# The opening of a two-block transformer kernel: the input in four column quarters between the halves of the first weights, those weights split by row blocks, products in another order

## What is computed

```python
h = rmsnorm(x, g_pre[i])        # x (1, 256, 1024); rmsnorm scales each row, then multiplies by the gain
proj = h @ w_in[i]              # w_in (1024, 3792)
(qa, ka, va, gate_a, qi, ki, wi, qb, kb, vb, fb, gate_b) = jnp.split(proj, offs, axis=-1)
```

## Time and profile before

| | us |
|---|---|
| median of 3 runs | 816.74 |
| lowest, highest | 814.30, 816.82 |
| the profiled execution, device time | 814.75 |
| its span | 812.9 |
| TensorE busy | 798.4 |

### The profile page before, as it was taken

How to read it: one execution, slowest core, us unless ns; L and a number is a source line. 1 busy time by engine, 2 the same in 40 slices (tenths; PEclk the granted TensorE clock), 3 DMA queues, 4 the chain that set the end, 5 groups by cost and what they waited for, 6 DMA issues and landing times.

```text
span 812.9 us, 11157 instructions
## 1 busy us (share of the span) xinstructions
PE 798.4 (98%) x4190; PEld 664.5 (82%) x4190; DVE 538.1 (66%) x728; ACT 415.6 (51%) x586; POOL 112.7 (14%) x144
## 2 busy tenths in 40 slices
PE   8999999999999999999999999999899999999998
PEld 6998987778878778888888888887567888888886
DVE  5647988767585766566656556677975766665661
ACT  5546556554655554364444444545665545444440
POOL 1600300000020510030000000079900000000000
PEclk9999999999999999999999999999999999999999
DMA  8951444346747633646655655464214466655541
GB/s 314 322 191 40 156 156 156 119 156 223 241 145 238 208 106 104 207 156 207 206 191 175 202 194 172 151 206 131 78 53 156 156 207 211 209 199 190 175 151 52
DMA packets 76503, 140.43 MB, mean 173 GB/s; under 512 B 2953, under 2 KB 22609, under 8 KB 76465
## 3 DMA queue, kind: packets, MB, share of 16 engines
q1 hardware_dynamic: 74352, 134.03, 49.8%
q0 software_dynamic: 1968, 5.82, 2.3%
q10 hardware_dynamic: 144, 0.07, 0.0%
HBM read 138.86 MB, written 1.05 MB: 172 GB/s over the span
## 4 chain that ended last, share of the span: by engine, by line
PE 90%; DVE 5%; ACT 2%; DMA 1%; issue 1%; POOL 0%; SPq 0%; ACTq 0%; DVEq 0%
PE bank L1737 56%; PE bank L2093 13%; PE bank L2095 7%; PE bank L1885 2%; PE bank L1803 2%; PE bank L2097 2%; DVE w_lo L1176 2%; PE bank L1946 2%; PE bank L1772 1%; PE bank L1855 1%; PE bank L1920 1%; DMA raw<-in_w_in 1%; DVE tok L1348 1%; PE bank L1751 1%; DMA raw<-in_w_mem_kv 1%
## 5 line engine op out<-in xcount | busy, mean ns | idle before, releaser
L1737 PE MATMUL bank<-w_hi,a_both 128*128 128x512 f32 (+2 forms) x752 | 233.6, 382 | 0.4 <-PE bank L1737 0.4
L1176 DVE TENSOR_TENSOR w_lo<-raw,w_hi 128x2048 fp32r<-128x2048 f32 (+2 forms) x65 | 146.0, 2247 | 53.8 <-ACT w_hi L725 53.3
L1615 DVE TENSOR_TENSOR w_lo<-raw,w_hi 128x2048 fp32r<-128x2048 f32 x48 | 110.0, 2292 | 91.9 <-ACT w_hi L1075 91.0
L2093 PE MATMUL bank<-a_both,w_hi 128*128 128x512 f32 x448 | 161.4, 399 | 0.0
L1737 PEld LDWEIGHTS bank<-w_hi,a_both 128*128 128x128 f32 x752 | 140.7, 188 | 22.0 <-issue 1.1
L725 ACT ACTIVATE w_hi<-raw 128x2048 fp32r<-128x2048 f32 (+2 forms) x64 | 120.7, 1888 | 59.7 <-PE bank L1737 35.6
L1075 ACT ACTIVATE w_hi<-raw 128x2048 fp32r<-128x2048 f32 x48 | 92.1, 1918 | 112.5 <-PE bank L1737 53.7
L1737 PE MATMUL bank<-w_hi,b_hi 128*128 128x512 f32 x376 | 148.7, 395 | 0.1
L1737 PE MATMUL bank<-w_hi,b_lo 128*128 128x512 f32 x376 | 146.5, 390 | 0.0
L1737 PE MATMUL bank<-w_lo,b_hi 128*128 128x512 f32 x376 | 146.5, 390 | 0.0
L1737 PE MATMUL bank<-w_lo,a_both 128*128 128x512 f32 (+2 forms) x376 | 141.7, 377 | 0.0
(11 more groups left out here) (242 smaller groups left out, 859.6 us busy)
## 6 DMA issues: line engine op xcount, KB each, us to landing
raw<-in_w_ff SPq DMA_DIRECT2D x64, 1024.0 KB, 5.1
raw<-in_w_in_moba SPq DMA_DIRECT2D x20, 512.0 KB, 4.4
raw<-in_w_merge SPq DMA_DIRECT2D x8, 1024.0 KB, 5.1
raw<-in_w_out SPq DMA_DIRECT2D x8, 1024.0 KB, 5.1
m<-in_w_in SPq DMA_DIRECT2D x6, 880.0 KB, 9.1
raw<-in_w_in SPq DMA_DIRECT2D x5, 880.0 KB, 8.5
raw<-in_w_mem_kv SPq DMA_DIRECT2D x4, 1024.0 KB, 5.2
raw<-in_w_ple_gate SPq DMA_DIRECT2D x4, 1024.0 KB, 5.0
```

The costliest lines, as they stand in the source:

```text
L1176: dve.tensor_tensor(w_lo[:, v % RING, 0:n], landing[land_slot(v)][:, 0:n], w_hi[:, v % RING, 0:n].bitcast(F32), ALU.subtract).then_inc(lo_ ...
L1615: dve.tensor_tensor(w_lo[:, (base + c) % RING, :], raw[:, (base + c) % RAW, :], w_hi[:, (base + c) % RING, :].bitcast(F32), ALU.subtract). ...
L1737: ins = pe.matmul(banks[t][:, 0:n], xa[:, kt, ts], wa[:, slot, w], start=first and k == 0 and q == 0, stop=last and k == kts - 1 and q == 2)
L2093: pe.matmul(b_hid[f][:, :].rearrange("p (q n) -> p q n", q=2), w_hi[:, slot, w], both_, start=kt == 0, stop=False)
```

## The change

- x comes in four column quarters instead of two halves by two token tiles: one transfer covers both token tiles of 256 columns, in 1 KB rows. Order on SP: quarter 0, row blocks 0 and 1 of unit 0, quarter 1 (its own semaphore `x_second_landed`), row blocks 2 and 3, quarters 2 and 3, then unit 1 as before.
- g_pre is loaded by ScalarE, behind the identity, instead of by GpSimd.
- ScalarE casts row blocks 0 and 1 of unit 0 in two instructions of 440 columns, and raises `half_ready` after each.
- TensorE transposes only group 0 ahead of the first products. Unit 0 then goes: hi products of row blocks 0 and 1; transposes of group 1; lo products of row blocks 0 and 1; hi, then lo products of row blocks 2 and 3; transposes of groups 2 and 3; w_lo products. Unit 1 keeps its order.

```diff
@@ -312,7 +312,7 @@
         memk_made, memq_made, moba_made = sem("memk_made"), sem("memq_made"), sem("moba_made")
         early_landed, half_rstd, x_half = sem("early_landed"), sem("half_rstd"), sem("x_half")
         half_landed, half_ready, pre_landed = sem("half_landed"), sem("half_ready"), sem("pre_landed")
-        x_upper_landed = sem("x_upper_landed")
+        x_upper_landed, x_second_landed = sem("x_upper_landed"), sem("x_second_landed")
         tile_done, x_tile = sem("tile_done"), sem("x_tile")
 
         merged, x_post, z_made = sem("merged"), sem("x_post"), sem("z_made")
@@ -501,21 +501,22 @@
                 for u in range(first, last):
                     load(u, land_slot(u), unit_source(u), unit_size(u))
 
-            def load_x(c):
-
-                for t in range(NT):
-                    sp.dma_start(x[:, t, c * CB:c * CB + CB], a["x"][0, t * P:(t + 1) * P, c * CB:c * CB + CB])\
-                        .then_inc((x_landed, x_upper_landed)[c], 16)
+            def load_x(q, landed_):
+
+                cols = slice(q * 2 * P, q * 2 * P + 2 * P)
+                sp.dma_start(x[:, :, cols], a["x"][0].rearrange("(t p) n -> p t n", p=P)[:, :, cols]).then_inc(landed_, 16)
 
             def load_first(k, landed_):
 
                 sp.dma_start(landing[0][:, k * CIN:(k + 2) * CIN].rearrange("p (k n) -> p k n", k=2),
                              unit_source(0)[:, k:k + 2, :]).then_inc(landed_, 16)
 
-            load_x(0)
+            load_x(0, x_landed)
             load_first(0, half_landed)
+            load_x(1, x_second_landed)
             load_first(2, raw_landed[0])
-            load_x(1)
+            load_x(2, x_upper_landed)
+            load_x(3, x_upper_landed)
 
             def mlp(base, lay):
                 w1 = a["w_ff1_2"][lay].rearrange("(k p) n -> p k n", p=P)
@@ -546,7 +547,6 @@
         @block.gpsimd
         def _(gp):
             link = Linker(gp, pool_chain)
-            gp.dma_start(pre_rows, a["g_pre"][0].rearrange("(k p) -> k p", p=P)).then_inc(pre_landed, 16)
             small = [(gain_rows[0:16, :], a["g_mix_2"].rearrange("l (k p) -> (l k) p", p=P)),
                      (gain_rows[16:32, :], a["g_mem_2"].rearrange("l (k p) -> (l k) p", p=P)),
                      (gain_rows[32:48, :], a["g_mlp_2"].rearrange("l (k p) -> (l k) p", p=P)),
@@ -946,13 +946,16 @@
 
 
             act.dma_start(ident[:], a["c_ident"]).then_inc(early_landed, 16)
+            act.dma_start(pre_rows, a["g_pre"][0].rearrange("(k p) -> k p", p=P)).then_inc(pre_landed, 16)
             act.sem_inc(free_a, 2)
             act.wait_ge(early_landed, 16)
             act.activation(ident_b[:], ident[:], ACT.Copy).then_inc(ident_made, 1)
 
             act.wait_ge(gains_made, 1)
             act.wait_ge(half_landed, 16)
-            act.activation(w_hi[:, 0, 0:2 * CIN], landing[0][:, 0:2 * CIN], ACT.Copy).then_inc(half_ready, 1)
+            for k in range(2):
+                w = slice(k * CIN, k * CIN + CIN)
+                act.activation(w_hi[:, 0, w], landing[0][:, w], ACT.Copy).then_inc(half_ready, 1)
             act.wait_ge(tr_hi, 1)
             group(G_H + 1, a_hi, 2, GAIN_PRE)
             act.wait_ge(raw_landed[0], 16)
@@ -1754,24 +1757,35 @@
 
             def product_by_terms(u, hi, lo, k0, banks, n):
 
-                pe.wait_ge(*((hi_ready, u + 1) if u else (half_ready, 1)))
-                for q, (xa, wa, split_of_x) in enumerate(((hi, w_hi, tr_hi), (lo, w_hi, tr_lo), (hi, w_lo, None))):
-                    if q == 2:
-                        pe.wait_ge(lo_ready, u + 1)
-                    for k in range(4):
-                        if u == 0 and q == 0 and k == 2:
-                            pe.wait_ge(hi_ready, 1)
-                        if u == 0 and q == 1 and k == 0:
-                            pe.wait_ge(x_upper_landed, 16 * NT)
-                            for g in range(2, 4):
-                                group(G_H + g, x, 2 * g)
-                        if split_of_x is not None and k % 2 == 0:
-
-                            pe.wait_ge(split_of_x, G_H + (k0 + k) // 2 + 1)
+                def term(q, ks):
+                    xa, wa = ((hi, w_hi), (lo, w_hi), (hi, w_lo))[q]
+                    for k in ks:
+                        if u == 0 and q == 0 and k < 2:
+                            pe.wait_ge(half_ready, k + 1)
+                        if q < 2 and k % 2 == 0:
+                            pe.wait_ge((tr_hi, tr_lo)[q], G_H + (k0 + k) // 2 + 1)
                         for t in range(NT):
                             ins = pe.matmul(banks[t][:, 0:n], xa[:, k0 + k, t * P:t * P + P], wa[:, u, k * n:k * n + n],
                                             start=k0 + k + q == 0, stop=k0 + k == D // P - 1 and q == 2)
-                ins.then_inc(unit_used, 1)
+                    return ins
+
+                if u == 0:
+                    term(0, (0, 1))
+                    pe.wait_ge(x_second_landed, 16)
+                    group(G_H + 1, x, 2)
+                    term(1, (0, 1))
+                    pe.wait_ge(hi_ready, 1)
+                    term(0, (2, 3))
+                    term(1, (2, 3))
+                    pe.wait_ge(x_upper_landed, 16 * 2)
+                    for g in range(2, 4):
+                        group(G_H + g, x, 2 * g)
+                else:
+                    pe.wait_ge(hi_ready, u + 1)
+                    term(0, range(4))
+                    term(1, range(4))
+                pe.wait_ge(lo_ready, u + 1)
+                term(2, range(4)).then_inc(unit_used, 1)
 
             def blocks_read(k):
 
@@ -2020,9 +2034,8 @@
             pe.wait_ge(early_landed, 16)
             pe.wait_ge(pre_landed, 16)
             pe.transpose(b_t[:, 0:8], pre_rows, ident[0:8, 0:8]).then_inc(gains_tr, 1)
-            pe.wait_ge(x_landed, 16 * NT)
-            for g in range(2):
-                group(G_H + g, x, 2 * g)
+            pe.wait_ge(x_landed, 16)
+            group(G_H, x, 0)
             pe.wait_ge(gains_made, 1)
             def in_pair(i, by_terms):
 
```

## The result

| | us |
|---|---|
| changed kernel, median of 20 runs | 817.74 (816.43 to 820.27) |
| kernel before, median of 20 runs beside them | 816.47 (814.30 to 817.55) |
| ratio, changed to before | 1.0024, 95% interval 1.0016 to 1.0033 |
| changed kernel's profiled execution, device time and span | 817.97, 816.2 |

The change makes the kernel slower by 0.24%, some 1.9 us, and the interval leaves out "no change". The forecast was 817.4 with +1.7 us. The 1.9 is the distance of the means (816.2 and 818.1); the medians are only 1.27 apart. Seven of the 20 times of the changed kernel stand apart from the others, at 819.1 to 820.3, above all of the kernel before; the mean of the other 13 is 1.2 above before's. Both profiled executions of the changed kernel (817.97, and 817.43 in run 12) lie in the lower group.

A forecast was written before the change was run, and what follows sets the result against it. TensorE, busy 98% of the span, bounds the kernel, with ScalarE's chain also setting unit 1's start. An earlier first product (-0.9 us) and later waits and transposes net +1.7, added to 815.65: 817.4, range 814.9 to 820.2.

The forecast's parts named there:

- First weights: Landing of unit 0's first two weight row blocks, 7.29 us before: 6.75 predicted, 6.2 by bytes, 7.3 by packets.
- a_hi of group 0: VectorE's first a_hi write, following the gain transpose at about 5.4: predicted from 6.3 to 7.2 us.
- Steps 1 to 6: Unit 0 after the first products: ScalarE waits for later transposes; upper ones start 1.73 us later, unit 1 at about 16.37.
- The sum: Start of unit 1: -0.9 us at the first product, two new waits and uncovered transposes, together +1.7, not given back.
- g_pre: Gain load on ScalarE's queue: lands at about 4.7 instead of 5.87 us, gain transpose at about 5.4, table load slips 0.4.
- Slow first weights: Rival, opening: packets or a slow first stretch hold the first weights to 7.3 to 8 us; +2.2 to +2.9, chance 0.17.
- TensorE's own queue: Rival, opening: only TensorE's queue bounds, casts do not; unit 1 at 13.6 us, -1.1, total 814.5, chance 0.05.
- The clock: Rival: TensorE's clock falls in the opening's new gaps, up to +1.7 us on top, 819.1, chance 0.06.
- two pairs: Four times of the kernel before: 814.3 and 814.75 in one pair, 816.74 and 816.82 in another; neither preferred.
- The covered case: Rival: the opening's loss is there but covered later, about 815.7 us; chance 0.12 shared with the clock's fall moving.
- the clock's fall near 579 moves: Other half of the covered rival: the clock's fall near 579 us moves and returns its 1.7; about 815.7, chance 0.12 shared.
- The base: Starting time for the forecast: mean of four executions, 815.65 us, rather than the profiled 814.75, giving 817.4.

The follow-up runs named there:

- run 12: Changed kernel, unchanged, profiled a second time: device time 817.43 us.
- run 2: Kernel before with only the x transfers in quarters in the changed order; g_pre, single cast and TensorE's order as before: ratio 0.9995.
- run 5: Changed kernel with group 1's transposes moved back ahead of the first products; upper transposes still behind all lo products: ratio 0.9991.
- run 6: Changed kernel with group 1's transposes ahead of the first products and the upper ones ahead of the hi products of row blocks 2 and 3: ratio 0.9985.
- run 1: Kernel before with only g_pre's transfer moved from GpSimd to ScalarE: ratio 1.0001.
- run 10: Changed kernel plus two products on zeros behind group 0's transposes and two in the wait for the cast of row blocks 2 and 3: ratio 1.0011.
- run 9: Kernel before plus two products on zeros behind the transposes of groups 0 and 1: ratio 0.9987 to the kernel before.
- run 3: Kernel before with only TensorE's order of unit 0 changed; transfers, g_pre and single cast as before: ratio 1.0031, 818.70 against 816.06 us.
- run 8: Kernel before, unchanged, profiled a second time: device time 817.91 us.
- run 4: Changed kernel with the eight upper transposes moved between the hi and lo products of row blocks 2 and 3: ratio 1.0005.
- run 7: As run 6, plus two products on zeros, one behind group 0's and one behind group 1's transposes: ratio 0.9980, median 814.26 us.
- run 11: As run 7, plus two more products on zeros ahead of the wait for the upper x: ratio 0.9985, median 815.64 us.

## Why the prediction was right

- **First weights.** Predicted 6.75 within 6.2 to 7.3; they landed at 6.03, outside my bounds on the early side, and at 5.73, 5.53 and 5.43 in other executions (runs 2, 5, 6). I took away bytes alone; the issue that falls away (they are issued at 1.23 instead of 1.65, so 0.42) stands ahead of them too. Run 1 against run 2 shows that it is what is queued ahead, not g_pre's queue. It cost nothing in the sum, since another bound took over.
- **a_hi of group 0.** Predicted ready at 7.2; VectorE began at 6.75 and ended at 7.63. The gain transpose went at 5.44 as predicted, but group 0's four loads took 0.71 and not 0.5 (0.42 in run 12). So the first products, predicted at 7.6, stood at 7.74 behind this, and not behind the weights. That the start was off by only 0.14 is luck: I had the landing 0.7 too late and a_hi 0.4 too early, and the bound passed from one to the other.
- **Steps 1 to 6.** Predicted against measured: group 1's transposes 8.35 and 8.44; lo products 8.85 and 8.96; idle 1.3 and 1.39; hi products of row blocks 2 and 3 10.89 and 11.05; upper transposes 12.35 and 12.55; copies 13.19 and 13.39; cast 14.63 and 14.83; wait ahead of unit 1 1.4 and 1.55; unit 1 16.37 and 16.57. The errors are 0.09 to 0.2, against 0.14 at the start: the durations and the two waits, which are the mechanism, came as written.
- **The sum.** +1.7 predicted; +1.87 at unit 1, +1.79 at unit 2 (21.27 against 19.48), +1.83 at 574 us, 2.05 between the filled kernels (runs 10 and 9), and 1.9 in the timed ratio, with 1.27 between the medians. The statement that it isn't given back holds. That the ratio comes so near is partly luck: it also holds the seven times at 819.1 to 820.3, and unit 1 starts at different times from one execution to the next, 1.77 apart in the kernel before (14.70 and 16.47) and 0.45 in the changed one (16.57 and 16.12).
- **g_pre.** By the Trainium skill, "DMA: Bandwidth & Descriptors", section "Issuing engines are not separate DMA queues", the move should save only issue time. In runs 3 and 8, with g_pre on GpSimd, it landed 3.9 after its issue instead of 4.6 and the gain transpose stood at 5.44 too. So the earlier trace rows had shown an execution with a late landing, and the 1.1 us between the queues that I read there is no fixed distance: nothing here speaks against the rule. The time to landing on ScalarE's queue is in no view; with the transpose at 5.44 it was 4.2 at most. ScalarE's table load slipped by 0.70 (1.25 to 1.95), not 0.4, and cost nothing, as I had said.
- **Rivals.** Slow first weights: did not come. TensorE's own queue: run 4 excludes it. The clock: it fell in neither profile of the changed kernel's opening, but it did in run 8, the kernel before, and in run 1; fillers take the same 0.13% off both kernels. I had it as an accident of the change with chance 0.06; it happens with either kernel's order, and can be part of the scatter that I had called two pairs. I can't rule it out for part of the executions of the changed kernel either: the price that I had set gave 819.1, seven of its times are at 819.1 to 820.3, none of the filled ones (run 10) is above 817.93, and no profile caught one of the seven. My "818 to 819.6 on either pair" for slow weights holds for the upper pair; on the lower it is 816.7 to 817.4.
- **The covered case:** excluded by the 574 us row. The other half of that rival, that the clock's fall near 579 moves, did come: neither profile of the changed kernel has it. It returned nothing, since the clock fell near 597 instead.
- **The base.** Adding to the mean of four executions rather than to the profiled one gave 817.4; on the profiled execution's own 814.75 the sum would have been 816.45, 1.3 below the median. The profiled execution was a fortunate one. The mean of the four was itself 0.8 below the median of the 20 (816.47), and +1.7 is 0.4 more than the medians differ by; so two errors of opposite sign leave the forecast 0.3 off. The lower end of the range is 815.0 by its own terms (814.53 + 0.5), not 814.9, which changes nothing.

## To carry to other kernels

A step that produces for another engine must be issued as early as its input is there, even if the queue that issues it is the bound: here TensorE's order decided when ScalarE could begin, and the products put ahead of the transposes cost more than the earlier first product won. Before moving a step behind others, follow the chain of the engine that it feeds to the next point where both meet, and look for the slack there (0.11 us here). And take a second profile of the kernel before when the effect is below the scatter of its runs.

## What the runs showed of the hardware that I had not expected

**The clock in the opening differs between executions of one kernel.** Kernel before: loads at the short durations throughout from the first products in one profile, the granted clock at 0.50 from 10 to 12 us in another, 1.77 us apart at unit 1, of which 0.46 are the landing of the weights. Two products on zeros in the gap took 0.13% off the time (interval 0.03 to 0.22%).

**The 1.4 us between 595 and 603 us.** The same two rows of products, in the kernel before and in the changed one:

```profile
593.73 0.93 PE L1885 MATMUL bank<-qk 64*128 64x128 f32 x8 [1.35 <-ACT prob L893]
599.75 0.93 PE L1885 MATMUL bank<-qk 64*128 64x128 f32 x8
```
```profile
595.38 0.93 PE L1899 MATMUL bank<-qk 64*128 64x128 f32 x8 [2.70 <-ACT prob L893]
602.94 0.93 PE L1899 MATMUL bank<-qk 64*128 64x128 f32 x8
```

The changed kernel is 1.65 behind at the first and 3.19 at the second. Between them its clock fell, and before's did not:

```profile
596.00:600.00 4.00, 4.00 (x27) 2.81 (x24) 1.50 (x7) 2.81 (x10) 0.00 (x0) 0.61 0.02 5
```
```profile
596.00:600.00 4.00, 4.00 (x28) 3.04 (x24) 2.57 (x11) 2.94 (x12) 0.00 (x0) 1.00 0.00 0
```

So the fall near 597 is the 1.4 us. Ahead of it TensorE had waited 2.70 instead of 1.35, and one cause of this wait is VectorE's split of the weights, 3.30 instead of the usual 2.28, beside GpSimd:

```profile
588.18 3.30 DVE L1179 TENSOR_TENSOR w_lo<-raw,w_hi 128x2048 fp32r<-128x2048 f32 x1 [1.22 <-ACT w_hi L725]
```
```profile
588.05 1.27 POOL L657 TENSOR_TENSOR m<-m 128x512 f32<-128x512 f32 x1
```

and in the kernel before, where it begins just behind GpSimd's instruction (586.21 + 1.26 = 587.47):

```profile
587.55 2.28 DVE L1176 TENSOR_TENSOR w_lo<-raw,w_hi 128x2048 fp32r<-128x2048 f32 x1
```

In the changed kernel GpSimd's instruction ends at 588.05 + 1.27 = 589.32; with 2.28 from there the split would end at 591.6, and it ends at 591.48. The Trainium skill, "SBUF — State Buffer", section "SBUF: two separate sides", states that a VectorE instruction with two SBUF inputs and a GpSimd instruction that reads SBUF take a shared port pair exclusively for the whole instruction, and that the later one blocks; this row agrees within 0.12 us, and the split is 1.02 us longer. The longer split by itself costs nothing that I can find: the changed kernel loses nothing up to 595.38, since the kernel before has its own fall at 579 to 583.

Over the 14 profiles the two things go together without an exception. Eight have a fall that begins between 576 and 586 us and a split of 2.28 (before, runs 2 to 7 and 10); six have none there and a split of 3.29 or 3.30 (the changed kernel, runs 1, 8, 9, 11, 12). Five of these six have a fall between 592 and 602 instead and the 1.4 us. The sixth is run 9, with a span of 813.0:

```profile
579.00:583.00 4.00, 4.00 (x32) 2.80 (x29) 3.70 (x13) 2.35 (x8) 3.64 (x5) 1.00 0.18 68
596.00:600.00 4.00, 4.00 (x26) 3.13 (x25) 2.63 (x10) 2.98 (x11) 0.00 (x0) 1.00 0.00 0
```

That an early fall keeps the two engines apart fits all of them; it wasn't tested by itself. Both kinds occur with the order of the kernel before (its first profile and run 8) and with that of the change (run 10 and run 12), so the 1.4 us is not a step of the change. How often each kind comes in the timed executions of either kernel isn't shown, and part of the 1.9 us in the ratio could be that.
